# A two-layer transformer block on one core: the down projections' seven products added up in PSUM, by two chains, over pairs of chunks

## The chip, the core and the metric

The program runs on one core of a Trainium2 chip. The metric is the device time in microseconds, the median of several executions. TensorE (PE) multiplies, VectorE (DVE), ScalarE (ACT) and GpSimd (POOL) work on what it leaves and prepare what it needs, SyncE (SP) issues most of the transfers. Each engine has a queue of its own, worked in order; they wait for each other by semaphores.

## What is computed

All in float32, 1024 tokens of width 1024. Only the two feed-forward parts matter here; the rest (a state-space mixer, a convolution, two attentions, a spatial gate, three merges) stays as it is.

```python
h = rmsnorm(x, g_pre_mlp)
ff = jnp.einsum('blf,fd->bld', jnp.square(jax.nn.relu(jnp.einsum('bld,df->blf', h, w_ff1))), w_ff2)
x = x + rmsnorm(ff, g_post_mlp)          # width D_FF = 4096
...
h = rmsnorm_2(x, norm2_g_2)
ff = (silu(h @ w_ffn_gate_2) * (h @ w_ffn_up_2)) @ w_ffn_down_2      # width D_FF_2 = 2816
x = rmsnorm_2(x + ff, final_g_2)
```

The lines of the second feed-forward are shortened.

## The kernel before

Every float32 product is made of three matmuls at the rate of rounded float32: each operand is split into a high part (`whi`, `h_hi`, written by ScalarE as a rounded copy) and a low part (the rest, by a subtraction), and high x high, high x low and low x high are added up in PSUM.

`FeedForward` (L1487) has an up phase and a **down phase**. f, the hidden activation, lies in DRAM in blocks of 256 features (`f_keep`), with Strassen-Winograd sums of its quarters (`s_keep`). The down projection takes f in chunks of 512 features. A chunk is a 2 x 2 block product, done with **seven products** in place of eight: `DOWN` names the sums of f's quarters, `TIMES` those of the weights' quarters (T1 to T4 are sums, B11, B21, B22 plain quarters). The first feed-forward has 7 chunks (49 products), the second 5 (35). What is left of f (two blocks of 256, or one) goes the plain way behind them: `pair` (16 tiles in two halves, L2184) or `alone` (L2170).

One product is 24 matmuls (L2159): four tiles of 128 features of the output's half, each in one PSUM bank, of 128x512. Product n uses four of the eight banks, product n + 1 the other four. So product n waits for the taking of product n - 2, the low part of its weights and the low part of its ring slot.

Per product the other engines do, in the step n of their loops:
- SyncE: `ring_load` (L1664) of the part of f for product n + 4 into one of four ring slots (0.5 MB), once product n is done; once a chunk `load_down` (L1549), 2 x 1 MB of weights into `raw`, when all parts of the chunk before are made.
- ScalarE: `ring_high` (L1676) for product n + 2; `down_hi` (L1632), the high parts of the next chunk's weights. It copies the first four products out of PSUM (`copy_product`, L1983).
- VectorE: `take_product` (L1993) of product n - 1, an addition of four banks, 128x2048, onto the sum of the same product of the chunks before; `ring_low` (L1680) for product n + 2; `down_sum` (L1604), the weight sums T1 to T4 of the next chunk, four a chunk, from steps 3, 5 and 6 of the chunk; and late `f_sum`s (L1698) of the last blocks of f in the first steps.
- GpSimd: `down_lo` (L1645), the low parts of the weights, seven a chunk.

The operands' places: nine or ten slots of 128x1024 twice (`place`, L1572), in `whi`, `wlo` and `dw`. The seven running products lie in seven arrays (`partial`, L1976): four in `xg`, three in `big`. After the last chunk VectorE **folds** them (`fold`, L2017) by seven or eight additions of 128x2048 into the four blocks of the output in `big`:

```python
"U2": (M6, M6, M1, 1, None), "U3": (M7, M7, M6, 2, "U2"), "U4": (M6, M6, M5, 3, "U3"),
"C11": (C11, C11, M1, 4, None), "C12": (C12, C12, M6, 5, "U4"), "C21": (C21, C21, M7, 6, "U3"),
```

In the first feed-forward five foldings come before the first `total` (L2082), the addition of a tile of `pair` onto `big`; in the second three stand between the totals of the last rows. There x itself (`x_keep`, 4 MB) is loaded into `big` at the start of the down phase, so that products are added onto it (`onto_x`). Behind the totals come the rows' norms, row by row; in the second feed-forward they end the kernel, with a store of each row.

The bank of tile t of `pair` is given by `bank(t)` (L2243), and for tiles 8 to 15 `before` (L2240) tells whose total must be done.

## Time and profile before

| | |
|---|---|
| median of 3 runs | 3348.96 us |
| lowest, highest | 3347.06, 3352.0 us |
| span of the profiled execution, first to last instruction | 3349.8 us |
| TensorE busy | 3268.0 us, 98%, 16,387 matmuls |
| VectorE, ScalarE, GpSimd busy | 2019.0, 1276.1, 1166.0 us |
| mean granted TensorE clock | 0.995 of full |
| moved by DMA | 378.76 MB, 113 GB/s in the mean |

The profile gives the span of its execution and no second time beside it; the span lies within the runs, 0.84 us above their median. Busy time of TensorE counts a matmul from its start to its modelled end, and these overlap: the distance of two starts, not the duration, is what a matmul costs in a row of them. A time line merges instructions of one form that follow each other (`x24`), and gives the idle time before and who ended it in brackets. The granted clock is that of TensorE as the chip allows it, 1.00 being 2.4 GHz, 0.50 being 1.2 GHz.

### The profile page before, as it was taken

To read this page: it belongs to the slowest core of one execution; us is meant where nothing else is said; L and a number is where in the kernel's file an instruction comes from. 1 tells how busy PE (TensorE), PEld (TensorE's weight loads), DVE (VectorE), ACT (ScalarE), POOL (GpSimd) and SP (SyncE) were. 2 spreads that over 40 slices of the span, in tenths; PEclk is the share of its full clock that TensorE was granted. 3 is DMA by queue.
4 is the path that set the end of the run, shared out by engine and by line. 5 is a ranking of instruction groups with operands and counts; after the bars stand their busy time and mean duration, and the time that the engine had idled before them with its cause. 6 is when DMAs were issued, how large, how long until landed. Compare 5 with 4: busy or idle time off the path is not lost.

```text
span 3349.8 us, 41139 instructions
## 1 busy us (share of the span) xinstructions
PE 3268.0 (98%) x16387; PEld 2698.4 (81%) x16387; DVE 2019.0 (60%) x2794; ACT 1276.1 (38%) x2024; POOL 1166.0 (35%) x487
## 2 busy tenths in 40 slices
PE   7999999999999999999999999999999999999998
PEld 6788877888888888787778888888887888888776
DVE  6883446543547676888943344445644376666788
ACT  4233434433136445434533333333332252333433
POOL 2343101444313444554012221222443244554543
PEclk9999999999999999999999999999999999999999
DMA  4233102335533444554321212222335233333643
GB/s 130 64 82 103 32 20 76 113 105 185 176 107 120 169 168 158 182 180 140 108 92 50 63 51 62 63 69 85 120 126 194 83 113 113 113 113 113 220 145 113
DMA packets 240746, 378.76 MB, mean 113 GB/s; under 512 B 22136, under 2 KB 180516, under 8 KB 227756
## 3 DMA queue, kind: packets, MB, share of 16 engines
q1 hardware_dynamic: 210172, 255.58, 23.9%
q10 hardware_dynamic: 26000, 109.81, 8.3%
q0 software_dynamic: 4384, 10.74, 0.9%
q8 instruction: 131, 2.15, 0.3%
q14 instruction: 59, 0.48, 0.0%
HBM read 263.66 MB, written 110.33 MB: 112 GB/s over the span
## 4 chain that ended last, share of the span: by engine, by line
PE 85%; DVE 8%; DMA 2%; ACT 2%; issue 2%; POOL 1%; SPq 0%; ACTq 0%; DVEq 0%; POOLq 0%
PE ps L1326 28%; PE ps L350 17%; PE ps L2159 8%; PE ps L841 5%; PE ps L305 3%; PE ps L1481 2%; PE ps L1483 2%; PE ps L1472 2%; PE ps L326 2%; PE ps L333 2%; PE ps L332 2%; PE ps L3829 2%; PE ps L3800 1%; PE ps L367 1%; PE ps L2201 1%
## 5 line engine op out<-in xcount | busy, mean ns | idle before, releaser
L297 POOL TENSOR_TENSOR wlo<-raw,whi 128x2048 fp32r<-128x2048 f32 (+1 forms) x85 | 297.6, 3502 | 878.6 <-ACT whi L289 878.2
L1326 PE MATMUL ps<-h_hi,own 128*128 128x512 f32 x1200 | 385.7, 389 | 0.0
L1326 PE MATMUL ps<-tb,whi 128*128 128x512 f32 x1200 | 369.4, 389 | 0.0
L350 PE MATMUL ps<-h_lo,whi 128*128 128x512 f32 x880 | 351.7, 400 | 0.4 <-POOL wlo L297 0.4
L350 PE MATMUL ps<-h_hi,wlo 128*128 128x512 f32 x880 | 344.3, 391 | 0.0
L996 POOL TENSOR_TENSOR own<-raw,own 128x1024 fp32r<-128x1024 f32 x50 | 139.7, 2794 | 424.2 <-ACT own L986 424.2
L2159 PE MATMUL ps<-dw,h_lo 128*128 128x512 f32 x1152 | 268.7, 393 | 11.0 <-DVE xg L2008 7.3
L1024 POOL TENSOR_TENSOR wlo<-wsum,whi 128x2048 fp32r<-128x2048 f32 x50 | 239.4, 4788 | 100.6 <-ACT whi L1019 100.6
L2159 PEld LDWEIGHTS ps<-dw,h_lo 128*128 128x128 f32 x1152 | 218.0, 190 | 59.0 <-issue 11.6
L1326 PEld LDWEIGHTS ps<-tb,whi 128*128 128x128 f32 x1200 | 225.2, 188 | 47.1 <-POOL wlo L1024 0.4
L1326 PEld LDWEIGHTS ps<-h_hi,own 128*128 128x128 f32 x1200 | 225.2, 188 | 46.7
L1237 DVE TENSOR_TENSOR pu<-pu,ps 128x512 f32<-128x512 f32 x170 | 116.6, 686 | 205.9 <-ACT fr L1142 185.0
L1326 PE MATMUL ps<-tb,wlo 128*128 128x512 f32 x600 | 233.4, 389 | 0.0
L1326 PE MATMUL ps<-h_lo,own 128*128 128x512 f32 x600 | 233.4, 389 | 0.0
L350 PE MATMUL ps<-h_hi,whi 128*128 128x512 f32 x880 | 228.9, 402 | 1.7 <-DVE cacc L2759 0.8
L289 ACT ACTIVATE whi<-raw 128x1024 fp32r<-128x1024 f32 (+1 forms) x87 | 127.7, 1468 | 256.7 <-PE ps L1472 113.5
L350 PEld LDWEIGHTS ps<-h_lo,whi 128*128 128x128 f32 x880 | 165.2, 188 | 41.4 <-issue 5.9
L350 PEld LDWEIGHTS ps<-h_hi,wlo 128*128 128x128 f32 x880 | 165.4, 188 | 32.6
L350 PEld LDWEIGHTS ps<-h_hi,whi 128*128 128x128 f32 x880 | 158.4, 188 | 39.5 <-issue 4.3
L3568 ACT ACTIVATE PB<-PB,OS 128x128 f32<-128x128 f32 (+1 forms) x192 | 85.0, 444 | 200.1 <-DVE OS L3699 200.1
L3633 POOL DMA_DIRECT2D dil_keep<-OS x96 | 52.0, 543 | 309.9 <-DVE OS L3706 309.9
L1683 DVE TENSOR_TENSOR h_lo<-xh,h_lo 128x1024 fp32r<-128x1024 f32 x84 | 132.1, 1572 | 35.1 <-ACT h_lo L1678 35.0
(419 smaller groups left out, 7438.0 us busy)
## 6 DMA issues: line engine op xcount, KB each, us to landing
raw<-in_w_ff_dram SPq DMA_DIRECT2D x32, 1024.0 KB, 5.5
raw<-in_w_in_dram SPq DMA_DIRECT2D x57, 512.0 KB, 4.5
raw<-in_w_in_dram SPq DMA_DIRECT2D x28, 1024.0 KB, 5.4
f_keep<-fr ACTq DMA_DIRECT2D x27, 1024.0 KB, 3.9
s_keep<-fr ACTq DMA_DIRECT2D x24, 1024.0 KB, 4.5
xh<-s_keep SPq DMA_DIRECT2D x48, 512.0 KB, 3.7
g_keep<-fr ACTq DMA_DIRECT2D x20, 1024.0 KB, 3.9
fr<-g_keep SPq DMA_DIRECT2D x20, 1024.0 KB, 5.1
```

The costliest lines, as they stand in the source:

```text
L289: nc.scalar.activation(whi[c % 2][:, 0:cols], raw[c % 2][:, 0:cols], ACT.Copy).then_inc(s_hi.sem, 1)
L297: nc.gpsimd.tensor_tensor(wlo[c % 2][:, 0:cols], raw[c % 2][:, 0:cols], whi[c % 2][:, 0:cols].bitcast(F32), ALU.subtract).then_inc(s_lo.se ...
L305: last = nc.tensor.matmul(out_, lhs(a, k), rhs(b, k), start=(k == 0 and n == 0), stop=(k == ks - 1 and n == 2))
L350: x = nc.tensor.matmul(ps[:, bank, :], w(a, k, m * P, P), H[b][:, k, sl], start=j == 0, stop=j == 23)
L841: return nc.tensor.matmul(ps[:, t, :], H[a][:, 4 * (j % 2) + k, t * P:(t + 1) * P], w[j](b, k, 0, HALF), start=start, stop=stop)
L996: nc.gpsimd.tensor_tensor(two(o), r[:, :, 0:P], two(h).bitcast(F32), ALU.subtract)
L1024: nc.gpsimd.tensor_tensor(wlo[c % 2][:, :], wsum[c % 2][:, :], whi[c % 2][:, :].bitcast(F32), ALU.subtract).then_inc(s_lo.sem, 1)
L1237: nc.vector.tensor_tensor(out_, u, ps[:, self.bank_of(i, a), :], ALU.add).then_inc(joined.sem, 1)
L1326: last = nc.tensor.matmul(ps[:, bank, :], w[p][:, k, :], x[r][:, k, :], start=k == 0 and q == 0, stop=k == 3 and q == 2)
L1683: nc.vector.tensor_tensor(self.ring(n, 1), self.ring(n, 1, True), self.ring(n, 0).bitcast(F32), ALU.subtract).then_inc(ring_lo.sem, 1)
L2159: last = nc.tensor.matmul(ps[:, self.bank_behind(4 * n + t), :], f[a][:, j, t * P:(t + 1) * P], w[:, b, (odd + j) % 2, :], start=j == 0 an ...
L3568: last = nc.scalar.activation(PB2[:, b % 2, h, lo:256], PB2[:, b % 2, h, lo:256], ACT.Exp, scale=-1.0, bias=OS[:, i % 2, b, h, HD + 1:HD + ...
```

## The change

All in `FeedForward`. (1) The seven products run in another order, and three of them begin a chain in PSUM, the others add onto what stands in their banks (`BEGIN`; matmuls with `start=False`): in banks of even products A11·B11, + S2·T2, + S3·T3, + A22·T4; in banks of odd ones S1·T1, + S4·B22, then A12·B21 anew. Every product's banks are taken onto one output block (`ONTO`), while the chain stays in the banks. (2) So the seven arrays and all foldings go, and `xg` is free: it holds the weights of two more chunks (`raw_of`), and `load_down` runs three chunks ahead. (3) The chunks behind the first run in **pairs** (`groups`, `seq`): product i of chunk c, then product i of chunk c + 1 onto the same banks, then one taking for both. K counts groups of products, 28 and 21. (4) ScalarE copies four takings (0, 1, 2, 6), VectorE takes the others. (5) Weight sums, high parts and low parts are made a fixed number of products ahead (`AHEAD`), one a step; T4 in two steps (T4a, T4). (6) x is loaded in four blocks of 1 MB into `fr` and added onto `big` by VectorE (`add_x`). (7) Nine places; the tiles of `pair` begin on the banks of the taking before the last.

```diff
-            DOWN = ("S2", "A11", "S3", "S1", "A12", "S4", "A22")
-            TIMES = ("T2", "B11", "T3", "T1", "B21", "B22", "T4")
+            DOWN = ("A11", "S1", "S2", "S4", "S3", "A12", "A22")
+            TIMES = ("B11", "T1", "T2", "B22", "T3", "B21", "T4")
+            BEGIN = (0, 1, 5)
+            ONTO = ("C11", "C22", "C12", "C12", "C22", "C11", "C21")
...
+            FIRST_PARTS = ("B11", "T1", "T2", "T3", "B22", "B21", "T4")
+            AHEAD = 5
...
                 self.chunks = (n - self.alone) // 2
                 self.N = 7 * self.chunks
-                self.u = take_units(nu + n)
+                self.places = 9
+                self.groups = [(0,)] + [(c, c + 1) for c in range(1, self.chunks, 2)]
+                self.seq = [(c, i) for g in self.groups for i in range(7) for c in g]
+                self.K = 7 * len(self.groups)
+                self.behind = [max(n for n, (c, i) in enumerate(self.seq) if c in self.groups[k // 7] and i == k % 7)
+                               for k in range(self.K)]
...
+            def raw_of(self, c):
+
+                if c % 3 == 0:
+                    return raw_pair[:, :, :]
+                return xg[:, 4 * (c % 3) - 4:4 * (c % 3), :].rearrange("p (u a) n -> p u (a n)", u=2)
...
+            def sums_of(self, n):
+
+                out_ = []
+                for ahead, names in ((self.AHEAD + 1, {1: ("T1",), 2: ("T2",), 4: ("T3",)}), (self.AHEAD + 2, {6: ("T4a", "T4")})):
+                    if 7 <= n + ahead < self.N:
+                        c, i = self.seq[n + ahead]
+                        out_ += [(c, x) for x in names.get(i, ())]
+                return out_
...
+            def copy_product(self, e, k):
+
+                self.product_done(e, self.behind[k])
+                for lo, hi, src in self.bank_runs(k):
+                    last = nc.scalar.activation(self.block_sum(self.ONTO[k % 7])[:, lo:hi, :], src, ACT.Copy)
                 last.then_inc(copied.sem, 1)
...
+            def taken_before(self, e, x, k):
+
+                self.product_taken(e, max(j for j in range(k) if self.ONTO[j % 7] == x))
+
+            def take_product(self, e, k):
+
+                x = self.ONTO[k % 7]
+                dst = self.block_sum(x)
+                self.product_done(e, self.behind[k])
+                self.taken_before(e, x, k)
+                if self.onto_x and self.behind[k] >= self.X_IN[self.X_ORDER.index(x)] + 4:
+                    e.wait_ge(x_added.sem, self.xa + self.X_ORDER.index(x) + 1)
+                for lo, hi, src in self.bank_runs(k):
+                    last = nc.vector.tensor_tensor(dst[:, lo:hi, :], dst[:, lo:hi, :], src, ALU.add)
                 last.then_inc(down_taken.sem, 1)
...
-                for x in names:
-                    out_, a, b, product_no, behind = {
-                        "U2": (M6, M6, M1, 1, None), "U3": (M7, M7, M6, 2, "U2"), "U4": (M6, M6, M5, 3, "U3"),
-                        "C11": (C11, C11, M1, 4, None), "C12": (C12, C12, M6, 5, "U4"), "C21": (C21, C21, M7, 6, "U3"),
-                        "C22": (C22, C22, M7, 3, "U3") if self.onto_x else (C22, M7, M5, 3, "U3"),
-                        "C22b": (C22, C22, M5, 3, "C22")}[x]
-                    self.product_taken(e, self.N - 7 + product_no)
-                    if behind:
-                        self.folded_at(e, behind)
-                    nc.vector.tensor_tensor(out_, a, b, ALU.add).then_inc(folded.sem, 1)
+            def add_x(self, e, j, k):
+
+                x = self.X_ORDER[j]
+                e.wait_ge(d_in.sem, self.x_in + 16 * (j + 1))
+                self.taken_before(e, x, k)
+                nc.vector.tensor_tensor(self.block_sum(x), self.block_sum(x), fr[:, 1, :, :], ALU.add).then_inc(x_added.sem, 1)
...
                 for n in range(self.N):
-                    c, i = n // 7, n % 7
-                    if n > 4:
-                        take(n - 1)
+                    k = self.behind.index(n - 1) if n - 1 in self.behind else None
+                    if k is not None and k not in (0, 1, 2, 6):
+                        self.take_product(e, k)
                     if n + 2 < self.N:
                         self.ring_low(e, n + 2)
                     if self.late_at(n):
                         self.f_sum(e, *self.late_at(n))
-                    if c + 1 == self.chunks:
-                        last_chunk(i)
-                    else:
-                        if i == 3:
-                            self.down_sum(e, c + 1, "T1", "T2")
-                        if i == 5:
-                            self.down_sum(e, c + 1, "T4")
-                        if i == 6:
-                            self.down_sum(e, c + 1, "T3")
+                    for c, x in self.sums_of(n):
+                        self.down_sum(e, c, x)
+                    if self.onto_x and n - 4 in self.X_IN:
+                        self.add_x(e, self.X_IN.index(n - 4), len([m for m in self.behind if m < n]))
+                    if n == self.N - 3:
+                        self.f_part_lo(e, 0)
+                    elif n == self.N - 2:
+                        self.alone_lo(e, 0)
                     if n in ROPE and not self.onto_x:
                         self.rope_dve(e, ROPE.index(n))
-                take(self.N - 1)
-                if self.onto_x:
-                    self.fold(e, "C12")
-                else:
+                self.take_product(e, self.K - 1)
+                if not self.onto_x:
+                    self.alone_lo(e, 1)
                     self.f_part_lo(e, 1)
-                    self.fold(e, "U4", "C11", "C22", "C21", "C12")
...
                 def chunk_product(n):
-                    c, i = n // 7, n % 7
+                    c, i = self.seq[n]
+                    k = next(k for k in range(self.K) if self.behind[k] >= n)
+                    first = c == self.groups[k // 7][0]
                     w, f = self.place(n), [self.ring(n, part) for part in range(2)]
                     ready, count = self.lo_of(c, self.TIMES[i])
                     e.wait_ge(ready.sem, count)
                     e.wait_ge(ring_lo.sem, self.go + n + 1)
-                    if n >= 2:
-                        self.product_taken(e, n - 2)
+                    if k >= 2 and first:
+                        self.product_taken(e, k - 2)
                     for t in range(4):
                         if n < 2:
                             self.bank_free_behind(e, 4 * n + t)
                         for j in range(2):
                             for q, (a, b) in enumerate(((0, 0), (0, 1), (1, 0))):
-                                last = nc.tensor.matmul(ps[:, self.bank_behind(4 * n + t), :], f[a][:, j, t * P:(t + 1) * P],
-                                                        w[:, b, (odd + j) % 2, :], start=j == 0 and q == 0, stop=j == 1 and q == 2)
-                                if i < 2 and t == 0 and j == 0 and q == 0:
+                                begins = first and i in self.BEGIN and j == 0 and q == 0
+                                last = nc.tensor.matmul(ps[:, self.bank_behind(4 * k + t), :], f[a][:, j, t * P:(t + 1) * P],
+                                                        w[:, b, (odd + j) % 2, :], start=begins, stop=j == 1 and q == 2,
+                                                        skip_group_check=True)
+                                if c % 3 == 0 and i < 2 and t == 0 and j == 0 and q == 0:
                                     last.then_inc(s_begun.sem, 1)
                     last.then_inc(down_product.sem, 1)
...
+            before = {8: 0, 9: 1, 10: 4, 11: 5, 12: 8, 13: 9, 14: 10, 15: 11}
             @staticmethod
             def bank(t):
-                return (4, 5, 6, 7, 0, 1, 2, 3)[t] if t < 8 else 4 + t % 4
+                return (4, 5, 2, 3, 6, 7, 0, 1)[t] if t < 8 else 4 + t % 4
```

The queues, as the programs lay them out. In each row: line, operation, output <- inputs, shape.

**VectorE, first chunk of the first down phase, steps 0 to 5.** `h_lo<-xh,h_lo` is `ring_low`, `fr<-fr` an f sum, `wsum`/`wfirst`/`dw_plain` a weight sum, L2006, L2008 and L2085 a taking. Before:

```order
L1683 TENSOR_TENSOR h_lo<-xh,h_lo 128x2x512 x3
L1708 TENSOR_TENSOR fr<-fr 128x512
L1683 TENSOR_TENSOR h_lo<-xh,h_lo 128x2x512
L1708 TENSOR_TENSOR fr<-fr 128x512
L1683 TENSOR_TENSOR h_lo<-xh,h_lo 128x2x512
L1708 TENSOR_TENSOR fr<-fr 128x512
L1617 TENSOR_TENSOR wfirst<-raw 128x1024
L1617 TENSOR_TENSOR dw_plain<-raw,wfirst 128x1024
L1683 TENSOR_TENSOR h_lo<-xh,h_lo 128x2x512
L1708 TENSOR_TENSOR fr<-fr 128x512
L2006 COPY big<-ps 128x4x512
```

After:

```order
L1749 TENSOR_TENSOR h_lo<-xh,h_lo 128x2x512 x5
L1679 TENSOR_TENSOR wsum<-xg 128x1024
L2085 TENSOR_TENSOR big<-big,ps 128x2x512 x2
L1749 TENSOR_TENSOR h_lo<-xh,h_lo 128x2x512
L1774 TENSOR_TENSOR fr<-fr 128x512
L1679 TENSOR_TENSOR dw_plain<-xg 128x1024
L2085 TENSOR_TENSOR big<-big,ps 128x4x512
L1749 TENSOR_TENSOR h_lo<-xh,h_lo 128x2x512
L1774 TENSOR_TENSOR fr<-fr 128x512
L1679 TENSOR_TENSOR dw_plain<-xg,wsum 128x1024
L2085 TENSOR_TENSOR big<-big,ps 128x2x512 x2
```

The f sums begin four steps in, the takings two products earlier (product 3 is VectorE's now), and a weight sum of chunk 1, read from `xg`, stands ahead of the first taking.

**VectorE, second group of products and on, in the first down phase.** Before, a taking stands between any two `ring_low`:

```order
L2008 TENSOR_TENSOR xg<-xg,ps 128x1024 x2
L1683 TENSOR_TENSOR h_lo<-xh,h_lo 128x2x512
L1708 TENSOR_TENSOR fr<-fr 128x512
L2008 TENSOR_TENSOR xg<-xg,ps 128x2048
L1683 TENSOR_TENSOR h_lo<-xh,h_lo 128x2x512
L2008 TENSOR_TENSOR xg<-xg,ps 128x1024 x2
L1683 TENSOR_TENSOR h_lo<-xh,h_lo 128x2x512
L1617 TENSOR_TENSOR dw_plain<-raw 128x1024
L1617 TENSOR_TENSOR wfirst<-raw,dw_plain 128x1024
L2008 TENSOR_TENSOR xg<-xg,ps 128x2048
```

After, between every second:

```order
L1749 TENSOR_TENSOR h_lo<-xh,h_lo 128x2x512
L2085 TENSOR_TENSOR big<-big,ps 128x4x512
L1749 TENSOR_TENSOR h_lo<-xh,h_lo 128x2x512 x2
L2085 TENSOR_TENSOR big<-big,ps 128x2x512 x2
L1749 TENSOR_TENSOR h_lo<-xh,h_lo 128x2x512
L1679 TENSOR_TENSOR wfirst<-raw 128x1024
L1749 TENSOR_TENSOR h_lo<-xh,h_lo 128x2x512
L1679 TENSOR_TENSOR dw_plain<-xg 128x1024
L2085 TENSOR_TENSOR big<-big,ps 128x4x512
```

**VectorE, the end of the kernel, from the last taking.** L2029 is a folding, L2090 and L2131 are totals. Before:

```order
L2008 TENSOR_TENSOR big<-big,ps 128x4x512
L2029 TENSOR_TENSOR big<-big,xg 128x4x512
L2090 TENSOR_TENSOR big<-big,ps 128x512 x2
L2029 TENSOR_TENSOR big<-big,xg 128x4x512
L2090 TENSOR_TENSOR big<-big,ps 128x512 x2
L529 RECIPROCAL nst<-nst 128x1
L2029 TENSOR_TENSOR big<-big,xg 128x4x512
L2090 TENSOR_TENSOR big<-big,ps 128x512 x2
L529 RECIPROCAL nst<-nst 128x1
```

After:

```order
L2085 TENSOR_TENSOR big<-big,ps 128x4x512
L2131 TENSOR_TENSOR big<-big,ps 128x512 x4
L530 RECIPROCAL nst<-nst 128x1
L2131 TENSOR_TENSOR big<-big,ps 128x512 x2
L530 RECIPROCAL nst<-nst 128x1
L2131 TENSOR_TENSOR big<-big,ps 128x512 x2
```

The foldings between the totals are gone.

## Rows read from the trace of the kernel before

**Rows 1.** The page, part 1: busy time of each engine over the whole span.

```profile
PE 3268.0 (98%) x16387; PEld 2698.4 (81%) x16387; DVE 2019.0 (60%) x2794; ACT 1276.1 (38%) x2024; POOL 1166.0 (35%) x487
```

**Rows 2.** Waits of TensorE: engine, line <- releaser: total us, times, longest us.

```profile
PE ps L2159 <- DVE xg L2008: 11.5, 4, 4.3
```

**Rows 3.** Time line of TensorE, first down phase: start, us; in brackets idle before.

```profile
1334.70 5.71 PE L2159 MATMUL ps<-whi,h_lo 128*128 128x512 f32 x24
...
1387.13 7.34 PE L2159 MATMUL ps<-dw,h_lo 128*128 128x512 f32 x24 [1.80 <-DVE xg L2008]
...
1563.64 8.46 PE L2159 MATMUL ps<-whi,h_lo 128*128 128x512 f32 x24 [4.29 <-DVE xg L2008]
...
1618.10 0.47 PE L2201 MATMUL ps<-whi,f_hi 128*128 128x512 f32 x1 [2.47 <-DVE big L2008]
```

**Rows 4.** Time line of TensorE, second down phase.

```profile
3114.42 5.70 PE L2159 MATMUL ps<-whi,h_lo 128*128 128x512 f32 x24 [0.70 <-issue]
...
3148.49 11.18 PE L2159 MATMUL ps<-dw,h_lo 128*128 128x512 f32 x48 [1.16 <-DVE big L2008]
...
3187.19 7.30 PE L2159 MATMUL ps<-dw,h_lo 128*128 128x512 f32 x24 [4.06 <-DVE xg L2008]
3194.32 5.60 PE L2159 MATMUL ps<-whi,h_lo 128*128 128x512 f32 x24
...
3314.00 0.39 PE L305 MATMUL ps<-whi,f_hi 128*128 128x512 f32 x1
```

**Rows 5.** Stretches: PE, PEld, DVE, ACT, POOL busy, clock, DMA share, GB/s.

```profile
1563.00:1566.00 3.00, 2.35 (x6) 1.90 (x7) 3.00 (x4) 1.29 (x2) 0.00 (x0) 0.50 0.00 0
1566.00:1572.00 6.00, 6.00 (x21) 4.76 (x20) 3.17 (x3) 0.00 (x0) 2.69 (x2) 0.71 0.00 0
```

**Rows 6.** Time line of VectorE before product 40 of the first phase.

```profile
1549.39 1.23 DVE L1683 TENSOR_TENSOR h_lo<-xh,h_lo 128x1024 fp32r<-128x1024 f32 x1 [4.07 <-ACT h_lo L1678]
...
1554.53 3.43 DVE L1617 TENSOR_TENSOR wsum<-raw 128x1024 f32<-128x1024 f32 x1
1558.07 3.23 DVE L1617 TENSOR_TENSOR dw_plain<-raw,wsum 128x1024 f32<-128x1024 f32 x1
1561.22 2.27 DVE L2008 TENSOR_TENSOR xg<-xg,ps 128x2048 f32<-128x2048 f32 x1
```

**Rows 7.** Time line of GpSimd in the same stretch.

```profile
1554.17 6.04 POOL L1654 TENSOR_TENSOR dw<-raw,dw 128x1024 fp32r<-128x1024 f32 x2 [9.28 <-ACT dw L1643]
```

**Rows 8.** Time line of VectorE at the end of the first phase.

```profile
1626.68 4.49 DVE L2029 TENSOR_TENSOR big<-big,xg 128x2048 f32<-128x2048 f32 x2
1631.30 1.41 DVE L2090 TENSOR_TENSOR big<-big,ps 128x512 f32<-128x512 f32 x2
...
1638.27 1.28 DVE L2090 TENSOR_TENSOR big<-big,ps 128x512 f32<-128x512 f32 x2
```

**Rows 9.** Time line of VectorE at the end of the kernel.

```profile
3327.36 3.73 DVE L2029 TENSOR_TENSOR big<-big,xg 128x2048 f32<-128x2048 f32 x1
...
3339.69 1.99 DVE L541 SCALAR_TENSOR_TENSOR big<-big,nst,gpb 128x1024 f32<-128x1024 f32 x1
3341.60 1.27 DVE L2090 TENSOR_TENSOR big<-big,ps 128x512 f32<-128x512 f32 x2
...
3344.61 1.29 DVE L541 SCALAR_TENSOR_TENSOR big<-big,nst,gpb 128x1024 f32<-128x1024 f32 x1
```

**Rows 10.** SyncE, start of the second down phase: the issue of a load.

```profile
3114.16 0.46 SPq L1753 DMA_DIRECT2D big<-x_keep  x1
```

**Rows 11.** Time line of ScalarE, start of the second down phase.

```profile
3132.22 1.06 ACT L1678 ACTIVATE h_lo<-xh 128x1024 fp32r<-128x1024 f32 x1 [4.18 <-DMA xh<-f_keep]
3133.18 1.87 ACT L1989 ACTIVATE xg<-ps 128x2048 f32<-128x2048 f32 x1
```

**Rows 12.** Time line of VectorE in the same stretch.

```profile
3137.17 0.68 DVE L1708 TENSOR_TENSOR fr<-fr 128x512 f32<-128x512 f32 x1
3138.72 1.23 DVE L1617 TENSOR_TENSOR wsum<-raw 128x1024 f32<-128x1024 f32 x1 [0.87 <-issue]
```

341 lines of the change are left out of this document (166 added, 175 removed).

## The prediction

> **What bounds the kernel now.** Read the busy shares first. TensorE works 3268.0 us, 98% of the span of 3349.8 [rows 1], and a change that leaves its 16,387 matmuls alone can win only where TensorE stands still, or behind its last matmul. Ask the waits of TensorE next. The longest group, as long as the wait for one of the first transfers, is one that this change touches: chunk products held back by VectorE's taking of an earlier product [rows 2]. Then the time line of TensorE through the two down phases. A product is 24 matmuls. From 3194.32 to 3314.00 us 22 of them run without a gap [rows 4]: 5.44 us each. The first phase lasts from 1334.70 to 1618.10 us, where the pair begins [rows 3]: 283.40 us for 49 products, which are 266.56 us; so 16.84 us are lost. The second lasts from 3114.42 to 3314.00: 199.58 us for 35 products, 190.40 us; 9.18 us are lost. I number the products of a phase from 0; product n is due 0.1 + 5.44n us after the phase's start.
>
> Where do these 26 us lie? Product 40 of the first phase waited 4.29 us, and then took 8.46 us where others take 5.60 [rows 3, 4]. The granted clock says why: 0.50 and 0.71 in the stretches after the wait, between the two levels or at the lower one (1.2 GHz), after TensorE had stood [rows 5]. So a long wait is paid for twice, here 4.48 + 2.87 = 7.35 us. The same is seen at product 9 (7.34 us long, behind 1.80 us) and at product 12 of the second phase, 4.23 + 1.69 us late [rows 3, 4]. Short waits (1.16 us, [rows 4]) cost themselves only. What VectorE did before product 40: two weight sums of 3.43 and 3.23 us, and only then the taking, 2.27 us, for which product 40 waited [rows 6]. Such a sum takes 1.23 us when GpSimd is idle [rows 12]; these two lie on GpSimd's 6.04 us of low parts [rows 6, 7]. Its queue had come late already, idle for 4.07 us until ScalarE had a ring part [rows 6].
>
> **The change, part by part.**
> *Takings.* Before, 76 of 84 products are taken by VectorE at 2.27 us (8 copied by ScalarE); now 41 (24 + 17) and 8. Fifteen foldings of 2.28 us go. Added are ten T4 sums at 1.23 us (6 + 4; T4 is made in two steps in chunks behind the first) and four additions of blocks of x at 2.28 us. VectorE: -35 x 2.27 - 15 x 2.28 + 10 x 1.23 + 4 x 2.28 = -92 us, in phases of 483 us. None of it is on the path in itself. What counts is the deadline. Before, product n waits for the taking of n-2: it must be done within 5.44 us of that product's end, 3.2 us of leeway. In a pair the next use of the same banks is one whole group of two products later: 10.88 us, 8.6 us of leeway. The largest lateness seen is 4.3 us, so the waits behind the first chunk go: product 33 (1.56) and 40 (7.35) of the first phase, product 9 (3.8 with its slow clock) and 8 (1.31), which fall in what is now the first pair; 12 of the second (5.92) and its waits at 6 to 8 (3.07). All of it, with 0.1 us at each start staying, is 16.84 - 2.63 - 0.1 = 14.1 us and 9.1 us.
> *End of the first phase.* The pair waited 2.47 us, 2.63 with the gap, for the last taking, since its first tile used that product's banks [rows 3]. The new bank order starts on the banks of the product before; six matmuls per tile, four tiles, 5.4 us, cover the last taking of 2.27. Gain 2.6 us. VectorE folded until 1631.2 and took tile 0 at 1631.30 [rows 8], nearly when TensorE had it, so TensorE's 2.6 us pass down the row pipeline behind. Tile 10 now waits for total 4, not total 2; TensorE needs it 16 x 1.36 + 2 x 2.72 = 27.2 us after the pair's start (1.36 us are six matmuls), and VectorE worked it at 1638.27, 20.2 us after that start [rows 8]: nothing.
> *End of the kernel.* Four foldings stood in VectorE's last queue, the last of 3.73 us [rows 9]. The last tile leaves TensorE at 3314.00 + 16 x 1.36 = 3335.8, about 3336.2 with its run-out; its total began only at 3341.60. Without foldings VectorE keeps pace to tile 11; each of the last rows then costs it 1.27 for the totals and 1.29 to 1.99 for the norm [rows 9] with some issue between, 2.7 to 3.4 us against TensorE's 2.72, so it is some 0.8 us behind at the end: 3337.0. Gain 4.6 us; bounds 3.0 (contention at each norm) and 6.0 (norm not late at all, last store free).
> *A new squeeze in the first chunk.* Products 0 to 2 are copied by ScalarE as before, but product 3 is now VectorE's, and a 4 MB load of the next two chunks' weights stands ahead of ring load 4. The second phase had such a load before: x_keep, 4 MB, issued at 3114.16 [rows 10]. Ring part 4 was then worked at 3132.22, and product 2 copied till 3135.05 [rows 11]. Now a weight part comes between, as large as the ring part of 1.06 us: copied till 3136.1, product 4 due at 3136.28, just met. Ring part 5 high till 3137.1, low till 3138.3; then T1 of chunk 1, which the queue has ahead of taking 3. Alone it is done at 3139.5 and taking 3 at 3141.8, with product 5 due at 3141.72: 0.1 us. Behind GpSimd's low part of chunk 2 it takes 3.43 us as in [rows 6], taking 3 ends at 3144.0, and product 5 waits 2.3 us; with the clock's fall of product 40 (2.87) the most is 5.2. I take 2.0 us a phase, near the busy-GpSimd end, since by ScalarE's order GpSimd starts that part just before the sum. The first phase has no 4 MB load before, but the same times from its start should hold.
>
> The Trainium skill bears on this sum (SBUF — State Buffer, Who interferes with whom): a VectorE instruction with two SBUF inputs and a GpSimd instruction that reads SBUF exclude each other for a whole instruction, whoever starts first, while one SBUF input contends with nothing. Rows 6 and 7 agree: 3.43 and 3.23 against 2.27 for the taking out of PSUM. By that rule the T1 sum is always blocked here and the total loses 0.6 us more than mine; by the undisturbed row of 1.23 us it would be 3.8 us better.
>
> *POOL and SP.* GpSimd has the same seven low parts a chunk, 6.04 us for two beside a busy VectorE [rows 7]: 21 of 38 us. SP's weight loads are issued three chunks ahead into xg and raw. Two of 2 MB fall together (products 15, 16), a ring load is given out four products ahead of its use, 21.8 us, less 2.3 for its two parts, and the latest one of rows 6 came 4.07 us behind VectorE's turn for it, two products ahead of its use. Nothing.
>
> **Sum.** 14.1 + 9.1 + 2.6 + 4.6 - 2 x 2.0 = 26.4 us. 3349.8 - 26.4 = 3323.4 for the profiled execution; the median of the runs, 3348.96, is 0.84 below its span, so **3322.5 us**.
>
> **Rivals.**
> A, *the start squeeze is at its worst*: product 4 waits for copy 2 and product 5 for taking 3 in both phases, 5.2 us each, and one of the queues passes it on to product 6 (another 2 us). 3322.5 + 2 x (3.2 + 2.0) = 3333. For it: f sums and the T2 sums follow in the same queue. Against: step by step VectorE has a taking of 2.27, a ring part like the sum of 1.23, an f sum of 0.68 and a weight sum of 1.23 [rows 12], 5.4 us for 5.44, so lateness is not passed on.
> B, *the takings were not the cause*: the lateness comes from ring transfers held up by 2 MB loads and from GpSimd, and meets product operands (low parts) in place of takings. Then only both ends gain: 3349.0 - 2.6 - 4.6 = 3341.8. For it: the 4.07 us wait in rows 6. Against: at product 40 the ring part was there in time, and the taking was last.
> C, *slower: GpSimd's queue locks*. The low part of T3 may run only when T4 is summed, and T4 now is summed after T3's turn in GpSimd's order. VectorE sums T4 of chunk 1 at product 12, T3 is needed at product 15: three products, 16.3 us, less 5 us of that step and 3.4 of the low part leaves 7.9 us. Is VectorE later than that, every pair of chunks (five) loses, say, the excess of 5 us and 2.87 of slow clock: 3322.5 + 39 = 3362. Against it: VectorE loses 92 us of work, and takings bind it to TensorE at every second product.
>
> **Chances.** Forecast 0.68, A 0.2, B 0.08, C 0.04. About 0.2% (6.7 us) can be told from no change here, so faster means below 3342.3: forecast and A and a part of B, 0.92; same 0.04; slower 0.04. The range runs from every unknown at its best (squeezes 0.1 us, end 6.0: 3322.5 - 3.8 - 1.4 = 3317.3) to A with a little over: 3317 to 3334.
>
> **What would show it.** TensorE's waits for takings drop from 14 us to at most 5, all at products 4 to 6 of a phase; the time from the first product to the next line's first matmul is about 268.7 us (first) and 192.5 us (second); no product behind the first chunk is longer than 5.7 us; the last total begins near 1 us after TensorE's end; no wait for a low part. It is wrong if a stretch behind product 7 shows a granted clock below 0.9, or if a wait for POOL stands on top.

## The result and the profile after

The changed kernel takes 3327.67 us (median of 4 runs, 3325.05 to 3331.32), the kernel before beside it 3349.72: 22 us less by these medians; the ratio of the runs is 0.9937, 95% interval 0.9923 to 0.9951, which is 21 us. Forecast were 3322.5 us with a range of 3317 to 3334. The profiled execution is the slowest of the four, 3331.32 us; its span is 3329.5, against 3349.8 before: 20.3 us less.

The page, part 1, and the engines' shares of the chain that ended last, after:

```profile
PE 3262.3 (98%) x16387; PEld 2695.8 (81%) x16387; DVE 1937.3 (58%) x2749; ACT 1278.2 (38%) x2023; POOL 1168.2 (35%) x487
...
PE 90%; DVE 4%; ACT 2%; DMA 2%; issue 1%; POOL 1%; SPq 0%; ACTq 0%; DVEq 0%; POOLq 0%
```

VectorE works 82 us less (2019.0 in [rows 1]; forecast 92). TensorE's waits, after (line waited for: total us, times, longest us), where [rows 2] had 11.5 us for one group of takings:

```profile
PE ps L2201 <- issue: 5.1, 2, 2.9
...
PE ps L2201 <- DVE big L2085: 0.3, 1, 0.3
```

Takings (L2085) hold it for 0.3 us in all. But 5.1 us stand as "issue" at the product line, two waits that were 0.1 and 0.70 us [rows 3, 4]. The time line of TensorE after, first the first phase, then the second (counts of x13, here, and of x16, x21 and x40, further on, only say that the stretch asked for ended inside a product):

```profile
1339.66 7.31 PE L2201 MATMUL ps<-wlo,h_lo 128*128 128x512 f32 x24 [2.27 <-issue]
...
1369.06 3.20 PE L2201 MATMUL ps<-whi,h_lo 128*128 128x512 f32 x13 [0.33 <-DVE big L2085]
...
1608.51 0.39 PE L2243 MATMUL ps<-whi,f_hi 128*128 128x512 f32 x1
...
3105.64 8.60 PE L2201 MATMUL ps<-wlo,h_lo 128*128 128x512 f32 x24 [2.87 <-issue]
```

Product 0 waits 2.27 and 2.87 us and then takes 7.31 and 8.60 us; undisturbed it takes 5.60. The stretches of 7 us from product 0 (PE, PEld, DVE, ACT, POOL busy, granted clock, DMA share, GB/s):

```profile
1339.66:1346.66 7.00, 7.00 (x24) 5.60 (x25) 3.29 (x5) 5.97 (x9) 0.00 (x0) 0.76 1.01 377
3105.64:3112.64 7.00, 7.00 (x18) 5.57 (x19) 6.13 (x8) 2.72 (x3) 0.64 (x1) 0.56 1.01 364
```

The granted clock is 0.76 and 0.56 in the mean of these stretches, between the two levels, after TensorE had stood. Why it stood is seen on VectorE and then on GpSimd ahead of the first phase:

```profile
1327.98 2.56 DVE L1679 TENSOR_TENSOR dw_plain<-raw,dw_plain 128x1024 f32<-128x1024 f32 x2
1330.45 3.42 DVE L1679 TENSOR_TENSOR wfirst<-raw 128x1024 f32<-128x1024 f32 x1
1333.79 2.26 DVE L1238 TENSOR_TENSOR pu<-pu,ps 128x512 f32<-128x512 f32 x3
...
1336.57 2.99 DVE L1749 TENSOR_TENSOR h_lo<-xh,h_lo 128x1024 fp32r<-128x1024 f32 x1
```

```profile
1329.35 6.79 POOL L1720 TENSOR_TENSOR dw<-dw_plain,dw 128x1024 fp32r<-128x1024 f32 x2 [4.12 <-DVE dw_plain L1679]
1336.11 2.37 POOL L1720 TENSOR_TENSOR whi<-wfirst,whi 128x1024 fp32r<-128x1024 f32 x1
```

Before, ScalarE made the high parts of B11 and T2 ahead of its copy of the last ups product; now it makes T1's there as well. So GpSimd has two low parts (L1720), T1's and T2's, while VectorE still has T3's sum to do: 3.42 us in place of 1.23 us. Then T3's low part lies on ring part 0, 2.99 us for 1.23 of work, and product 0 needs that ring part. In the second phase T3's sum takes 3.42 us as well, and T3's low part lies on an f sum just ahead of ring part 0, 2.34 us for 0.69 of work.

Placed on the landmarks, the 20.3 us are: first phase, first matmul to the pair, 283.40 to 268.85, -14.55; second phase 199.58 to 193.40, -6.18; from the last chunk product to the end 35.80 to 30.46, -5.34; the two start waits, +4.34; all other code, +1.4. That last term is chance in part: at 152 us, in code that the change does not touch, this execution waits 4.29 us for a low part of GpSimd (L351), where the profiled executions of the kernel before and of the runs below wait 0.3 us or less. So the profiled execution is no typical one, and the medians are the measure of the change.

### The profile page after: what moved, and what is told of

Its sections match the earlier page's. It is cut to its first block, busy times and chain, and to the rows that moved or that the text cites. A ratio compares the mean times of both kernels' runs of the same rounds, so it can differ in the third digit from the quotient of the medians.

```text
span 3329.5 us, 41035 instructions
## 1 busy us (share of the span) xinstructions
PE 3262.3 (98%) x16387; PEld 2695.8 (81%) x16387; DVE 1937.3 (58%) x2749; ACT 1278.2 (38%) x2023; POOL 1168.2 (35%) x487
## 4 chain that ended last, share of the span: by engine, by line
PE 90%; DVE 4%; ACT 2%; DMA 2%; issue 1%; POOL 1%; SPq 0%; ACTq 0%; DVEq 0%; POOLq 0%
PE ps L1327 27%; PE ps L351 17%; PE ps L2201 13%; PE ps L842 5%; PE ps L306 3%; PE ps L1482 2%; PE ps L1484 2%; PE ps L1473 2%; PE ps L327 2%; PE ps L334 2%; PE ps L333 2%; PE ps L3871 2%; PE ps L3842 1%; PE ps L368 1%; PE ps L2243 1%; PE ps L3350 1%
## 5 line engine op out<-in xcount | busy, mean ns | idle before, releaser
L351 PE MATMUL ps<-h_lo,whi 128*128 128x512 f32 x880 | 352.3, 400 | 4.6 <-POOL wlo L298 4.6
L351 PE MATMUL ps<-h_hi,wlo 128*128 128x512 f32 x880 | 344.8, 392 | 0.0
L2201 PE MATMUL ps<-dw,h_lo 128*128 128x512 f32 x1104 | 253.3, 389 | 0.0
L2201 PEld LDWEIGHTS ps<-dw,h_lo 128*128 128x128 f32 x1104 | 207.3, 188 | 43.0
L351 PE MATMUL ps<-h_hi,whi 128*128 128x512 f32 x880 | 228.9, 402 | 1.7 <-DVE cacc L2801 0.9
L351 PEld LDWEIGHTS ps<-h_lo,whi 128*128 128x128 f32 x880 | 165.5, 188 | 46.1 <-issue 5.9
L351 PEld LDWEIGHTS ps<-h_hi,wlo 128*128 128x128 f32 x880 | 165.8, 188 | 32.6
L351 PEld LDWEIGHTS ps<-h_hi,whi 128*128 128x128 f32 x880 | 158.4, 188 | 39.6 <-issue 4.3
L1749 DVE TENSOR_TENSOR h_lo<-xh,h_lo 128x1024 fp32r<-128x1024 f32 x84 | 139.2, 1657 | 51.9 <-ACT h_lo L1744 51.9
L1744 ACT ACTIVATE h_lo<-xh 128x1024 fp32r<-128x1024 f32 x84 | 88.8, 1058 | 207.1 <-DMA xh<-s_keep 110.2
```

What stands on the lines that cost most here:

```text
L351: x = nc.tensor.matmul(ps[:, bank, :], w(a, k, m * P, P), H[b][:, k, sl], start=j == 0, stop=j == 23)
L1744: nc.scalar.activation(self.ring(n, 0), self.ring(n, 1, True), ACT.Copy).then_inc(ring_hi.sem, 1)
L1749: nc.vector.tensor_tensor(self.ring(n, 1), self.ring(n, 1, True), self.ring(n, 0).bitcast(F32), ALU.subtract).then_inc(ring_lo.sem, 1)
L2201: last = nc.tensor.matmul(ps[:, self.bank_behind(4 * k + t), :], f[a][:, j, t * P:(t + 1) * P], w[:, b, (odd + j) % 2, :], start=begins, s ...
```

## The experiments

Times stand beside runs of the kernel before on the same chip (3350.3 to 3351.0 us in median, 3349.72 beside the changed kernel), so a difference to the changed kernel is good to 1 or 2 us and smaller ones rest on the traces. Four questions: what removed the waits behind the first chunk, what removed the pair's wait, what the start costs, and what the foldings and GpSimd's order are worth.

**Pairs undone** (single_groups)

```diff
-self.groups = [(0,)] + [(c, c + 1) for c in range(1, self.chunks, 2)]
+self.groups = [(c,) for c in range(self.chunks)]
```

> The changed kernel with every chunk a group of its own: products taken one by one (49 and 35 groups of banks in the two phases in place of 28 and 21), the two PSUM chains, the direct takings, the T4 sums in two steps and the weights loaded three chunks ahead stay. It asks what the pairs alone do. Theory of the forecast (pairs give VectorE 8.6 us of leeway in place of 3.2, and that is what removed the waits behind the first chunk): 35 takings of 2.27 us come back, the deadline is 5.44 us again, and waits for takings come back behind product 6, with a stretch of fallen clock behind the long ones: 12 to 20 us more in the two phases, and 2.6 us more at the start of the pair of the first phase, since with 49 groups the first tiles meet the banks of the last one: 3342 to 3350. Rival (not the pairs: the lateness came from the foldings, from all four weight sums in a row and from weights that arrived one chunk ahead, and these are gone here too): no wait behind product 6 is over 1 us, only the 2.6 us at the pair come: about 3330.

Measured: 3332.97 us, ratio to before 0.9948 [0.9934, 0.9962]. In the whole time line of TensorE's two phases there is no wait for a taking; only the pair waits:

```profile
1337.44 7.30 PE L2201 MATMUL ps<-wlo,h_lo 128*128 128x512 f32 x24 [2.27 <-issue]
...
1608.78 0.47 PE L2243 MATMUL ps<-whi,f_hi 128*128 128x512 f32 x1 [2.47 <-DVE big L2085]
```

The second phase lasts 193.42 us, as with pairs (193.40). The rival holds: the pairs did not remove the waits. Nor did less work on VectorE: the stretches of the first phase, here and then in the kernel before, have nearly the same VectorE work (third sum, 242.23 and 246.08 us), but TensorE stands for 2.5 us of the one (the pair) and 11.1 us of the other:

```profile
1337.44:1608.78 271.34, 268.80 (x1177) 221.69 (x1177) 242.23 (x165) 119.83 (x114) 121.05 (x45) 0.99 0.52 179
```

```profile
1334.70:1618.10 283.40, 272.30 (x1177) 223.44 (x1177) 246.08 (x161) 118.17 (x116) 129.79 (x46) 0.98 0.50 172
```

**Single groups with two sums in a row** (single_groups_sums_together): as single_groups, but the sums of T1 and T2 of each later chunk stand one right behind the other.

```diff
-{1: ("T1",), 2: ("T2",), 4: ("T3",)}
+{1: ("T1", "T2"), 4: ("T3",)}
```

The theory put on record was that two sums in a row bring waits for takings of 1 to 4 us back, 5 to 15 us over the 3333 of single_groups; the rival was no wait and 3333 again. Measured: 3332.36 us, ratio to before 0.9947 [0.9934, 0.9961]. Four short waits for takings come back, 2.0 us in all (0.67, 0.65 and 0.52 at products 11 to 13 of the first phase, 0.18 at product 7 of the second), and the time is that of single_groups. So making the sums one by one is worth 2 us of wait at most here, and the long waits do not come back without it.

**Sums of a chunk apart, in the kernel before** (before_sums_apart)

```diff
 if i == 3:
-    self.down_sum(e, c + 1, "T1", "T2")
+    self.down_sum(e, c + 1, "T1")
+if i == 4:
+    self.down_sum(e, c + 1, "T2")
```

> The kernel before, with one line changed: the weight sums of T1 and T2 of the next chunk stand behind two different takings (fourth and fifth product of a chunk) and not one right after the other. The run with single groups has no wait for a taking behind the first chunk, so the pairs' leeway is not what removed them; this run asks whether the two sums in a row were the cause. Theory: yes. Between two takings VectorE then has at most one blocked sum of 3.4 us and a ring part, 3.4 + 1.2 + 2.3 = 6.9 us at worst against 5.44 with 3.2 of leeway: the waits of 4.29, 1.40 (first phase) and 4.06 us (second) and their slow clock (2.87 and 1.69) go, 12 to 16 us: 3333 to 3338. Rival (the ring part that comes late behind the weights' load is the cause): the waits stay above 2 us and the time at 3345 or more.

Measured: 3352.26 us, ratio 1.0009 [1.0000, 1.0018]: no gain. The long waits that the theory named, 4.29, 1.40 and 4.06 us, are gone. But in the first phase eight waits of 0.2 to 1 us stand in their place, two of them for GpSimd's low parts (0.96 and 0.95); product 6 now waits 2.69 us in the first phase (before, nothing) and 4.90 us in the second (before, 1.16); and the pair waits 3.16. So the forecast of the time is rejected, while the two sums in a row were a part of the long waits.

**Ring part first, in the kernel before** (before_ring_part_first)

```diff
-if i == (2 if c == 0 else 0):
-    ...
 self.product_done(e, n)
 if n + 4 < self.N:
     self.ring_load(e, n + 4)
+if i == (2 if c == 0 else 0):
+    ...
```

> The kernel before, with SP's order changed alone: in the product at which the next chunk's weights (2 MB) are loaded, the ring load of four products ahead is issued first and the weights behind it. Theory of the late ring part: before, ScalarE waited 8.9 us for the ring part behind the weights (3.5 us is usual in the run with single groups), and VectorE 4.1 us for ScalarE; both go, and with them the waits of product 40 and 12 and of products 9 and 33: 3333 to 3338. Rival (the sums in a row): VectorE comes to the two sums earlier, but they still take 6.7 us together; since GpSimd's low parts start with them, the waits fall by no more than half: 3340 to 3346.

Measured: 3345.04 us, ratio 0.9984 [0.9975, 0.9993], 5.3 us less. There is no wait behind product 9 of either phase: products 33 and 40 of the first and 12 of the second no longer wait. So the late ring part was a cause there. It was one of two that met, since the run before took the same waits away with the loads as they were. SyncE and then ScalarE of the kernel before, ahead of product 40:

```profile
1538.16 0.89 SPq L1552 DMA_DIRECT2D raw<-in_w_ff_dram  x2
1539.15 0.41 SPq L1673 DMA_DIRECT2D xh<-f_keep  x1
```

```profile
1548.30 1.06 ACT L1678 ACTIVATE h_lo<-xh 128x1024 fp32r<-128x1024 f32 x1 [8.86 <-DMA xh<-f_keep]
```

The two loads of 1 MB are issued just ahead of the ring load, and ScalarE waits 8.86 us for it; its high part is done 4.36 us ahead of product 39, which needs it. How long ScalarE stands is not in itself the measure: after the edit it still waits up to 8.35 us for a ring part (single_groups: 4.97 us in the first phase, 5.88 in the second; the changed kernel: 7.35). What counts is how far ahead of its product the part is ready, and behind product 9 that is 6.2 us or more after the edit. Even that does not decide alone: in the changed kernel one part is ready only 4.83 us ahead of product 20, and no taking is waited for.

What the edit costs is product 6. It now waits 4.53 us in the first phase (before, nothing) and 4.95 in the second (before, 1.16), and each time products 6 to 8 take 2.8 us more than 16.48, so most of the gain is lost again. In the first phase:

```profile
1373.38 19.32 PE L2159 MATMUL ps<-dw,h_lo 128*128 128x512 f32 x72 [4.53 <-DVE big L2006]
```

Here the first weights come later than before, and VectorE stood 4.47 us (before, 1.34) ahead of chunk 1's sums; a sum of 3.29 us and a ring part of 3.40 us, both held, then stand ahead of the taking.

**Both edits** (before_both_orders)

> The kernel before with both edits of the runs before_ring_part_first and before_sums_apart: ring load ahead of the weights' load, and the T1 and T2 sums behind different takings. Theory (VectorE's takings, single as before, hold TensorE only where two things fall together, a late ring part and sums that GpSimd holds; with both spread out single takings are in time, as in the run with single groups): the stalls behind the first chunk fall under 3 us in all, and there remain the last taking at the pair (2.5), the first chunk's wait (about 4.5) and the folds at the end: 3336 to 3341. Rival (the sums apart alone made nothing, 3352; the edits do not add): 3344 to 3348, as the ring part first alone.

Measured: 3347.73 us, ratio 0.9992 [0.9982, 1.0001]. The edits do not add, and the time lies in the rival's range. Behind product 9 there are only waits of 0.3 us left, three in all; product 6 waits 4.41 and 5.56 us. Why the first chunk gets worse in the kernel before whenever these queues are reordered was not tried apart.

**Old order of banks at the pair** (old_tile_banks)

```diff
-before = {8: 0, 9: 1, 10: 4, 11: 5, 12: 8, ...}
+before = {8: 0, 9: 1, 10: 2, 11: 3, 12: 8, ...}
-return (4, 5, 2, 3, 6, 7, 0, 1)[t] if t < 8 else 4 + t % 4
+return (4, 5, 6, 7, 0, 1, 2, 3)[t] if t < 8 else 4 + t % 4
```

> The changed kernel with the order of banks for the sixteen last tiles of the first phase as it was before (bank 4 to 7, then 0 to 3, and tile 10 freed by total 2). Theory: the pair's first tile asks for a bank of the last product and waits for its taking, 2.3 to 2.6 us, and perhaps some slow clock behind it: 3330 to 3331, and the stretch from the end of the last chunk product to the pair's first matmul grows from 0 to 2.5 us. Rival: VectorE and ScalarE set the pace of the rows behind the pair, so the wait is there but the time does not move (within 0.5 us).

Measured: 3327.84 us, ratio 0.9934 [0.9920, 0.9947], and no wait at the pair. Both theories miss. The two runs together tell why: with 49 groups (single_groups) the new order waits 2.47 us, as the old order did before [rows 3]; with 28 groups the old order does not wait. Consecutive groups alternate between two halves of the banks; an odd count ends in the half in which the tiles begin, an even one in the other. The number of groups removed the wait, not the order.

This run also shows what the start hides. TensorE, first phase, and the granted clock of the same 7 us as above:

```profile
1338.04 5.70 PE L2201 MATMUL ps<-wlo,h_lo 128*128 128x512 f32 x24 [2.27 <-issue]
...
1367.30 3.92 PE L2201 MATMUL ps<-whi,h_lo 128*128 128x512 f32 x16 [1.80 <-DVE big L2085]
```

```profile
1338.04:1345.04 7.00, 7.00 (x31) 5.80 (x32) 3.27 (x5) 5.98 (x9) 0.00 (x0) 1.00 1.02 384
```

After the same wait of 2.27 us the clock stayed at its upper level in this execution. Product 0 took 5.70 us, and product 5 then waited 1.80 us for the taking behind chunk 1's T1 sum, the squeeze that the forecast had put at 2.0. In the second phase, after 2.87 us, the clock stayed up too, and product 5 waited 0.44 us. In the profiled run of the changed kernel the slow clock had covered most of this. The first phase comes to the same length in both: 268.85 and 268.74 us.

**A later T1 at the start** (first_high_parts_behind_copy)

```diff
 def act_last(self, e):
-    self.down_hi(e, 0, "B11", "T1", "T2")
+    self.down_hi(e, 0, "B11")
 def act_last_joins(self, e):
-    self.down_hi(e, 0, "T3")
+    self.down_hi(e, 0, "T1")
     self.ring_high(e, 0)
 def act_last_join(self, e):
     self.ring_high(e, 1)
+    self.down_hi(e, 0, "T2")
```

T3's high part goes to product 0, ahead of B22 and B21.

> Only ScalarE's queue at the start of a phase is changed: of the first chunk's weights it makes B11 high alone before the copy of the last ups product, T1 high behind that copy and then the first ring part, T2 high behind the second ring part, T3 high at product 0. So GpSimd is idle while VectorE does the four weight sums. Theory (GpSimd's low parts, let in early, hold VectorE and so product 0): VectorE's T3 sum falls from 3.42 to 1.23 us in both phases; T1 low still begins about when ring part 0 is due and may hold it by up to 2.2 us, so product 0's wait of 2.27 and 2.87 us falls to 0.1 to 1.5 us, and with it the slow clock of product 0 (7.3 and 8.6 us long, 5.6 undisturbed): 3320 to 3325. Rival (the ring's transfer or the joins set product 0): its wait stays at over 2 us and the time at 3327.7.

**T3's sum behind ring part 0** (first_sum_and_high_parts_behind): as above, but T1 high stays in `act_last`, and `dve_last` makes the sums of T1, T2 and T4 alone, T3's behind `ring_low(0)`.

> As the run before, and VectorE makes T3's sum behind the first ring part, with T1 high in its early place (so T1's low part runs beside VectorE's joins, which read PSUM and one SBUF operand). Theory: nothing of VectorE's way to the first ring part is held: joins begin on ScalarE's copy, ring part 0 takes 1.23 us, product 0 waits at most 0.3 us in both phases and takes 5.6 us. Gain at product 0: 2.2 + 1.8 and 2.6 + 3.0 us, 9.6. If nothing else moves: 3318. What I expect in part (the forecast's squeeze in the first chunk, which the late start may have hidden): taking 3 is held by the T1 sum of chunk 1, so 0.5 to 2.5 us a phase of a wait for a taking appear at product 5: 3319 to 3323. Rival: the time stays at 3327.7 since later work only waits longer.

Measured: 3329.68 us (0.9939 [0.9925, 0.9952]) and 3329.26 us (0.9936 [0.9923, 0.9950]): no gain, though the mechanism is right. In the second, product 0 waits for nothing in either phase and takes 5.60 and 5.69 us. But then:

```profile
1349.49 5.69 PE L2202 MATMUL ps<-dw,h_lo 128*128 128x512 f32 x24 [1.25 <-ACT big L2070]
...
1368.63 6.63 PE L2202 MATMUL ps<-whi,h_lo 128*128 128x512 f32 x21 [2.11 <-DVE big L2086]
...
3112.71 12.75 PE L2202 MATMUL ps<-dw,h_lo 128*128 128x512 f32 x48 [2.03 <-DVE h_lo L1749]
```

Product 2 waits for ScalarE's copy, product 5 for the taking (2.11 us; 2.08 in the other run), product 1 of the second phase for its ring part. With a wait of 0.41 us at product 1 and one of 0.22 at product 4 that makes five, 6.0 us in all, and two of them (2.11 and 2.03) are followed by 1.7 us of slow clock each. What had been a late start came back as waits further on. In the first of the two runs it came back the same way: product 0 waits 0 and 0.42 us, and five waits hold later products for 6.9 us.

**Smaller loads and ScalarE's order too** (start_loads_and_order): `load_down(1)` behind ring load 1 and `load_down(2)` behind ring load 4 in place of both ahead of it; high parts B22, T3, B21 one per product; T1's sum of chunk 1 behind taking 3.

> The changed kernel with a new start of both phases. Kept from the run before: T3's sum behind ring part 0. New: the first weights' load of 4 MB is cut in two (chunk 1 behind ring load 1, chunk 2 behind ring load 4), ScalarE makes one weight part per product in the first three (B22, T3, B21), so copy 0 to 2 come sooner, and the T1 sum of chunk 1 stands behind taking 3. Theory (the late start only hid the squeeze of the first chunk, whose cause is the 4 MB load ahead of ring load 4, ScalarE's queue and the blocked sum): product 0 waits 0 to 0.4 us, products 2 to 5 at most 0.5 us each, no slow clock: phases of 267 and 191.5 us from the first matmul, 9 us less than the changed kernel from the end of ups to the end of a phase: 3318 to 3320. Rival (the DMA engines set it, 4 MB and five ring parts however ordered): ring part 2 or 5 comes late in its place and 1 to 3 us of wait stay in each phase: 3323 to 3328.

Measured: 3328.30 us, ratio 0.9934 [0.9920, 0.9947]. Products 0 and 2 to 5 wait no more, product 1 of the first phase 0.41 us; product 6 waits 2.60 and 0.93 us, since the sums of T1 of chunks 1 and 2 now stand together ahead of taking 4. Product 1 of the second phase waits 2.13.

**No two held operations together** (start_spread)

```diff
 def dve_last(self, e):
-    self.down_sum(e, 0, *self.W_SUMS)
+    self.down_sum(e, 0, *self.W_SUMS[:3])
-for c, x in self.sums_of(n):
+for c, x in () if n == 3 else self.sums_of(n - 1 if 4 <= n <= 7 else n):
     self.down_sum(e, c, x)
 if self.onto_x and n - 4 in self.X_IN:
-FIRST_PARTS = ("B11", "T1", "T2", "T3", "B22", "B21", "T4")
+FIRST_PARTS = ("B11", "T1", "T2", "B22", "T3", "B21", "T4")
```

T3's sum stands behind `ring_low(1)`. The cut loads stay; ScalarE makes B22, then T3, then B21 and T4 at products 0 to 2, and the first high parts of the pair at products 3, 4 and 5.

> A version meant to beat both kernels: the changed kernel with the start of both phases spread out. Against the run start_loads_and_order: T3's sum of chunk 0 stands behind ring part 1, in the second phase ring part 1 stands ahead of the last joining; the sums of the first pair of chunks (T1, T1, T2, T2) each stand one product later, never two together; the high parts of B11 of chunks 1 and 2 and of T1 are made one product later. Theory (each wait left in the first chunk has a single held VectorE operation before it, 2.60 and 0.93 us at product 6, 2.13 at product 1, and after a wait over 2 us the clock falls): waits in the two phases sum to under 1.5 us, first matmul to pair 267 to 268.5 us, second phase 191 to 192: 3318 to 3321. Rival (what is taken from one wait comes back at the next product, as it did in the three starts tried so far): the ups' end to the phase's end stays 271 and 194 to 196 us: 3325 to 3329.

(The ring part moved ahead of the last joining was that of the first phase; the text above says the second.)

Measured: **3320.50 us**, 3318.23 to 3322.41, ratio to before 0.9910 [0.9895, 0.9924]. The best of all kernels here, 7 us under the changed one, and its slowest run is faster than the fastest of the changed kernel. The starts of both phases:

```profile
1333.27 5.60 PE L2214 MATMUL ps<-wlo,h_lo 128*128 128x512 f32 x24
...
3094.28 5.71 PE L2214 MATMUL ps<-wlo,h_lo 128*128 128x512 f32 x24
3100.87 9.33 PE L2214 MATMUL ps<-dw,h_lo 128*128 128x512 f32 x40 [0.89 <-issue]
```

0.89 us at product 1 of the second phase is the only wait of both. They last 266.81 and 191.65 us against 266.56 and 190.40 of pure products: 1.5 us are left to gain in them. The edit moves several operations at once; which of the moves was needed was not tried apart.

**Foldings put back** (dummy_folds): four additions of `fr[:, 1]` to itself, 128x2048, ahead of total 0 and behind totals 1, 3 and 5.

> The changed kernel with four additions of 128x2048 put back on VectorE where the foldings stood at the end of the kernel (before total 0 and behind totals 1, 3 and 5); they work on a free buffer and leave the output as it is. Theory (the foldings in VectorE's last queue were the 5.5 us of the tail): totals begin 3 to 4 us later than TensorE's tiles, tail from the last chunk product to the end 34.5 to 36 us in place of 30.3, and the time 4.2 to 5.7 us up: 3332 to 3333.4. Rival (norms, their contention with GpSimd or the last store set the end): the tail grows by less than 1.5 us.

Measured: 3331.80 us, ratio 0.9945 [0.9928, 0.9961], 4.1 us more than the changed kernel; the tail is 3329.0 - 3294.51 = 34.5 us against 30.5, so +4.0: the tail is at the lower end of the theory, the time 0.2 us under it. The runs of the two kernels overlap a little (3330.30 to 3333.36 beside 3325.05 to 3331.32), so the tail is the firmer figure. The foldings in the last queue were most of the 5.34 us. The additions here took 2.29 us each, and none was held to the 3.73 of [rows 9], as the last folding was; those 1.4 us are about what is missing, which is an estimate and was not tried apart.

**Rival C forced** (hi_three_ahead)

```diff
-AHEAD = 5
+AHEAD = 3
```

(and a guard that starts the later high parts at the eighth).

> The changed kernel with AHEAD = 3 in place of 5: high parts are made three products ahead, sums of T1 to T3 four ahead, T4's five ahead. It forces rival C of the forecast: T3's low part stands in GpSimd's queue until T4 is summed, now at the end of the product before the one that needs T3. Theory C as priced there (5 us and 2.87 us of slow clock per group of a pair, five groups): 39 us, 3367; since the second T3 of the pair waits as well, up to 60 us: 3355 to 3390, with waits of TensorE for POOL at the ninth and tenth product of each group. If a low part, a sum and a ring part still fit into a product, the waits are under 1 us each: 3328 to 3335.

Measured: 3357.05 us, ratio 1.0021 [1.0012, 1.0031], 29 us over the changed kernel. TensorE's waits:

```profile
PE ps L2201 <- POOL dw L1720: 12.6, 6, 4.4
...
PE ps L2201 <- POOL wlo L1720: 5.8, 2, 3.4
...
PE ps L2201 <- POOL whi L1720: 0.9, 1, 0.9
```

19.3 us of waits for low parts, single ones up to 4.4 us, and some 8 us of slower products behind them. In each of the five pairs of chunks the product that needs the second T3 waits, 2.5 to 4.4 us. VectorE, GpSimd and TensorE at the first of them:

```profile
1425.69 1.23 DVE L1679 TENSOR_TENSOR dw_plain<-dw_plain 128x1024 f32<-128x1024 f32 x1
...
1427.06 3.19 POOL L1720 TENSOR_TENSOR dw<-dw_plain,dw 128x1024 fp32r<-128x1024 f32 x1 [5.94 <-ACT dw L1708]
...
1430.30 12.70 PE L2201 MATMUL ps<-dw,h_lo 128*128 128x512 f32 x48 [3.38 <-POOL dw L1720]
```

T3's low part starts 0.14 us behind the end of T4's sum, for which the program makes it wait (the profile names ScalarE, which ended last by a little), and product 16 starts when it is done. So the mechanism of rival C is real: at a distance of three products this change would have lost more than it won.

## Why the prediction came out right, and where it did not

The time lies in the range, and the waits behind the first chunk went as forecast. The reason given for that was wrong, the start waits were missed, and two errors inside the phases made up for each other. Its own terms, and what was measured:

- **Waits behind the first chunk, -14.1 and -9.1 us.** All of them went, as said. With the 2.6 of the pair and 2.0 of squeeze the phases were to last 268.7 and 192.5 us; they last 268.85 and 193.40. The cause given, "in a pair the next use of the same banks is one whole group of two products later ... 8.6 us of leeway", is wrong as the cause: without any pair there are no waits either. Before, a late ring part (the weights' load of 2 MB stood ahead of its load) and two held sums in a row met in VectorE's queue. Taking either away removed the long waits behind product 9, and neither gained more than 5.3 us, since product 6 then waited. The prediction had the 4.07 us row [rows 6] and gave it to rival B. Rival B was right about this cause and wrong in its conclusion, since the change moves these loads and sums as well. The sums one by one are not what does it in the changed kernel (single_groups_sums_together: 2.0 us of waits with two in a row). Which of the rest does it (weights loaded three chunks ahead, high parts five products ahead, the T4 sum in two steps, the new order) was not tried apart and stays open.
- **End of the first phase, -2.6.** The wait of 2.47 us went. The step "the new bank order starts on the banks of the product before; six matmuls per tile, four tiles, 5.4 us, cover the last taking" names the wrong cause: the even number of groups did it.
- **The squeeze, +2.0 a phase at product 5.** Measured in the first phase: 0.33 us in the profiled run, 1.80 where the clock held, 2.11 where the start was free. In the second: nothing, 0.44 (0.66 in dummy_folds) and nothing. Place and cause (the T1 sum held to 3.42 us, as the row of 3.43 said) were right. The size was right for the first phase and three times too large or more for the second. The rule of the Trainium skill (SBUF — State Buffer, Who interferes with whom), by which that sum is held whenever a low part of GpSimd runs, agrees with the trace: 3.42 and 3.43 us in the two phases of the changed kernel.
- **The step that failed** is "with 0.1 us at each start staying". The change puts one more high part, T1's, ahead of the copy of the last ups product in ScalarE's queue, so one more low part of GpSimd falls on T3's sum, and T3's own falls on ring part 0 (first phase) or on the f sum ahead of it (second). That is 2.27 and 2.87 us of wait and, in the profiled run, 1.7 and 3.0 us of slow clock. The same rule of the Trainium skill would have pointed to it; the prediction applied it to one sum and not to the queue ahead of product 0. Taking the low parts away from the start removed both waits (0 in both phases in first_sum_and_high_parts_behind), which shows the cause. The error is 4.3 us of wait.
- **End of the kernel, -4.6.** Measured -5.34. The last pair of totals began 1.2 us after TensorE's last matmul ended (3320.96), near the 1 us said; before, it was 5.7 us (3341.60 and 3335.93). That is 4.5 us, and 0.85 us lie behind the last norm, in the store of the row. The time line of VectorE there:

```profile
3316.36 3.29 DVE L542 SCALAR_TENSOR_TENSOR big<-big,nst,gpb 128x1024 f32<-128x1024 f32 x1
...
3322.15 1.28 DVE L2131 TENSOR_TENSOR big<-big,ps 128x512 f32<-128x512 f32 x2
...
3325.17 1.28 DVE L542 SCALAR_TENSOR_TENSOR big<-big,nst,gpb 128x1024 f32<-128x1024 f32 x1
```

- **The sum.** The phases and the tail were forecast at -26.4 and measured at -26.1 in the profiled execution. That this agrees so well is luck: 4.0 us of squeeze were forecast and 0.33 came, while 4.7 us of slow clock at the two products 0 (1.71 and 3.00) were not forecast. The 5.8 us between -26.1 and -20.3 are the two start waits (4.34) and 1.4 elsewhere. The median is off by 5.2 us, and the start waits are most of that.
- **Rival C**, 5 us and slow clock per group, 39 us: forced, it cost 29. Here the forecast had the mechanism right and the price a third too high.

## What to carry to other kernels

A change that loosens one deadline usually moves other things too: undo the named cause alone, with the rest kept, before believing it. Here neither the pairs nor the bank order did what they were credited with. When a queue is moved ahead, look at what else then stands beside it on the other engines, above all at the first operation of the next stage. Waits in a full stretch of one engine are easily handed on and not removed: four starts gave 3327.7 to 3329.7 us, and only the fifth, which spread the sums, the high parts and the loads over the first products, gave 3320.5.
